# Router ranking in two products, expert rows loaded in halves and turned at once, second layer norm from sum and mean square

## Chip, cores and metric

The kernel runs on one core of one Trainium2 chip. The metric is the device time of one execution in microseconds (us); lower is better. Engines are named as the profile names them: PE (TensorE), DVE (VectorE), ACT (ScalarE), POOL (GpSimd), SP (SyncE, which issues transfers and nothing else here); PEld is PE's weight load.

## What is computed

Two transformer-like blocks on 512 tokens of width 1024, all in float32. The change lies in the first block, between its mixing part and the second block. Cut to that:

```python
xl = post_norm(xl, mod_l[2] * out_l, ln1_g, ln1_b)          # layer_norm(ALPHA * x + y)
hl = modulate(xl, mod_l[3], mod_l[4])                       # input of the experts
# hier_moe: 4 groups of 8 experts
grp = argmax(hl @ w_rg + b_rg)                              # group of each token
top_v, top_i = top_k(le[grp], 2)                            # its two experts
w = p_grp * softmax(top_v)
order = argsort(flat_e)                                     # 1024 (token, expert) pairs by expert
y = swiglu(rows of each expert, w_eg[e], w_eu[e], w_ed[e])
yl = segment_sum(y * w)                                     # sum of each token's two rows
xl = post_norm(xl, mod_l[5] * yl, ln2_g, ln2_b)
# second block: x + 0.5 * swiglu(rms_norm(x)), mixing, x + 0.5 * swiglu(rms_norm(x))
```

`layer_norm` subtracts the mean over the 1024 features and divides by the root of the mean squared deviation plus 1e-5.

## The kernel before, in words

**Layout.** The residual `XT` lies features by tokens: 8 tiles of 128 features x 512 tokens. One tile operation is therefore 128x512. A product in full precision is made of three products of split operands (`HTh`/`HTl`, `HLB`): high x high, high x low, low x high (L582 to L584).

**Weights.** Weights come in tiles of 512 KB through a ring (`Weights`). SP loads them into 4 slots `raw`, and during the expert stage into 5 more, `more` (`lend`, `take_back`). ACT makes the high half of a tile (`ring.hi`, L291), DVE the low half (`ring.lo`, L302), four tiles ahead of PE. A slot is free again when DVE has made the low half, and SP waits for that.

**Order.** Each engine runs its own list of instructions in order, with semaphore waits. The functions `pe_...`, `act_...`, `dve_...` and `pool_...` of one stage are written separately; the order in each function is the order on that engine.

**End of the mixing part** (`*_branches`, last loops). For the eight output tiles `wo`, PE makes the product, DVE adds it to `XT`, and the first layer norm and the router's logits are gathered beside it. `moved(k)` subtracts the mean from tile k on DVE (L2215); POOL then multiplies each tile by the reciprocal deviation `RA` (L2749, signal `xn`); ACT makes from it `HF`, the experts' input (L1570), and the scaled residual (L1572).

**Router** (`*_router`). PE turns the logits (L984). DVE finds the group, the two experts and their one-hot sum `ohs` (L2248 to L2283). PE ranks the pairs in each expert: for token tile i, the strictly lower triangle `sU` times `ohs[i]` plus `ones` times all earlier tiles, and the counts (`rank`, L991 and L994: 14 products of 32 columns). DVE turns ranks into blocks and slots (L2288 to L2346), with one more product (L1004). Meanwhile PE turns `HF` into rows (L680), ACT copies them (L1577) and stores them in DRAM (`H2`, shown as h_scratch). The result `ix` holds the rows that POOL gathers for each expert. SP waits for the last store of `H2` and then loads the five `more` tiles.

**Experts** (`*_experts`). For expert j PE turns the gathered rows `XG` (L1019), makes the gate and up products (L1048 to L1050) and the down product of the expert before (L1030 to L1032). POOL gathers two experts ahead (L2759) and scatters the results to `YD` (y_scratch, L2768). A conditional part for overfull experts follows.

**Combine** (`*_combine`). POOL waits for the last scatter and loads `YD` back in four transfers of 1 MB into `YI` (L2788). For each token tile ACT scales the first row (L1639) and DVE adds the scaled second one (L2406). When all four are done, PE turns the rows (L1072) and DVE adds them to `XT` (L2410) and sums the tiles (L2099). One product with a matrix of 1/1024 gives the mean (L870), DVE subtracts it (L2105), the squares of the centred tiles are added in pairs and go through four products (L854), ACT makes the reciprocal root (L1450, L1452), and DVE, ACT and DVE make the input of the feed-forward part, tile by tile (L2418, L1648, L1650, L2426).

**Feed-forward part** (`*_ffn`). 2 x 11 pairs of products, each pair 48 matmuls. The sum of squares for its RMS norm is made on ACT and POOL (L1660, L2796); `pe_rms` (L864) waits for it behind the first pair.

Of the kernel before, what the change touches and what calls it, by code (L numbers as in the profile page):

```python
# [11 lines left out]
ALU = mybir.AluOpType  # L12
# [8 lines left out]
NRAW = 4  # L21
# [282 lines left out]
def build(nc, I, outT, counted):  # L304
# [5 lines left out]
    with ctx:  # L310
# [22 lines left out]
        y_in = [signal(f"y_in{i}", 16) for i in range(4)]  # L333
# [140 lines left out]
        YL = here("YL", [128, 4, 1024])  # L474
# [52 lines left out]
        PRD = rc(4, 2, 32)  # L527
        LE = rc(NOV, 32)
# [318 lines left out]
        def pe_statistics(i):  # L847

            bank = psum.take(pe, ("square", i))

            def sums():
                for j in range(4):
                    pe.wait_ge(*dve_out.when(("square", i, j)))
                    mm(bank[:, :], K("o1024"), TMP[2 + j % 2][:, :], start=(j == 0), stop=(j == 3)).then_inc(  # L854
                        *pe_out.next(("square", i, j)))
                    yield

            return sums()

# [6 lines left out]

        def pe_norm(i):
            bank = psum.take(pe, ("mean", i))
            pe.wait_ge(*dve_out.when(("mean", i)))
            mm(bank[:, :], K("o1024"), SQ[:, :], start=True, stop=True).then_inc(*pe_out.next(("mean", i)))  # L870
            squares = pe_statistics(i)
            for j, _s in enumerate(squares):
                if j == 2:
                    psum.give(("mean", i), dve_out, ("centred", i, 7))
            psum.give(("square", i), act_out, ("ln", i))
# [104 lines left out]
        def pe_router():  # L980
# [7 lines left out]
            pe.wait_ge(*dve_out.when("ohs"))  # L988
            for i in range(4):
                for j in range(i + 1):  # L990
                    mm(bank[:, i * 32:(i + 1) * 32], K("sU") if j == i else K("ones"), ohs[:, j, :],  # L991
                       start=(j == 0), stop=(j == i))
            for j in range(4):
                ins = mm(bank[:, 128:160], K("ones"), ohs[:, j, :], start=(j == 0), stop=(j == 3))  # L994
            ins.then_inc(*pe_out.next("rank"))
# [70 lines left out]

        def pe_combine():
            for k in range(8):
                bank = psum.take(pe, ("yl", k))
                pe.wait_ge(*dve_out.when(("yl", 3)))  # L1070
                for i in range(4):
                    ins = transpose(bank[:, cols(i)], YL[:, i, cols(k)], K("ident"))  # L1072
# [381 lines left out]
        def act_squares(i, k, signal, done):  # L1454

            if k % 2:
                return
# [1617 lines left out]
```

## Time and profile before

| | us |
|---|---|
| median of 3 runs | 2786.14 |
| the three runs | 2785.41, 2786.14, 2793.68 |
| the profiled execution, its own time | 2790.24 |
| its span | 2788.6 |
| PE busy | 2565.5 (92%) |
| DVE busy | 1686.8 (60%) |
| ACT busy | 1219.4 (44%) |
| POOL busy | 300.7 (11%) |

A page of the profile gives the busy time of each engine, the busy share in 40 slices of the span, the DMA queues and the chain of work that ended last. The busy time of an engine says how much work there is; the chain says which work the end waited for. The timeline shows single instructions with start and duration, and in square brackets how long the engine had been idle before one and what ended that. The windows view sums stretches and has the clock granted to PE, as a share of its full speed.

### The profile page before, as it was taken

To read this page: it belongs to the slowest core of one execution; us is meant where nothing else is said; L and a number is where in the kernel's file an instruction comes from. 1 tells how busy PE (TensorE), PEld (TensorE's weight loads), DVE (VectorE), ACT (ScalarE), POOL (GpSimd) and SP (SyncE) were. 2 spreads that over 40 slices of the span, in tenths; PEclk is the share of its full clock that TensorE was granted. 3 is DMA by queue.
4 is the path that set the end of the run, shared out by engine and by line. 5 is a ranking of instruction groups with operands and counts; after the bars stand their busy time and mean duration, and the time that the engine had idled before them with its cause. 6 is when DMAs were issued, how large, how long until landed. Compare 5 with 4: busy or idle time off the path is not lost.

```text
span 2788.6 us, 30655 instructions
## 1 busy us (share of the span) xinstructions
PE 2565.5 (92%) x12058; PEld 2033.4 (73%) x12058; DVE 1686.8 (60%) x2315; ACT 1219.4 (44%) x1640; POOL 300.7 (11%) x261
## 2 busy tenths in 40 slices
PE   5999898897899959999999948999999998999999
PEld 3867667586778747888888835888887766788887
DVE  3476575857645758999999955434443555543442
ACT  2322323222335448888888835222243544422221
POOL 0010111102122321111111001000023000100000
PEclk9999999999899969999999968999999978999999
DMA  6224242322346329999999941232232110232322
GB/s 262 89 69 154 68 140 99 119 94 69 104 147 204 122 101 327 359 366 363 365 370 364 352 156 61 81 110 97 76 126 69 53 38 23 76 101 80 114 77 82
DMA packets 144885, 427.13 MB, mean 153 GB/s; under 512 B 21152, under 2 KB 35744, under 8 KB 143840
## 3 DMA queue, kind: packets, MB, share of 16 engines
q1 hardware_dynamic: 118560, 373.24, 38.3%
q0 software_dynamic: 13504, 26.64, 2.8%
q10 hardware_dynamic: 12672, 25.24, 2.5%
q8 instruction: 97, 1.59, 0.2%
q14 instruction: 52, 0.43, 0.0%
HBM read 414.55 MB, written 35.65 MB: 161 GB/s over the span
## 4 chain that ended last, share of the span: by engine, by line
PE 75%; DVE 13%; ACT 6%; DMA 3%; issue 2%; POOL 1%; ACTq 0%; SPq 0%; POOLq 0%; DVEq 0%
PE bank L582 16%; PE bank L584 16%; PE bank L583 15%; PE bank L1048 4%; PE bank L1050 4%; PE bank L1049 4%; PE bank L1032 2%; PE bank L1030 2%; PE bank L1031 2%; DVE CA L1999 2%; DVE tmp L1893 2%; ACT HLB L291 1%; DVE HLB L302 1%; DMA early<-in_wada 1%; PE bank L1019 1%
## 5 line engine op out<-in xcount | busy, mean ns | idle before, releaser
L302 DVE TENSOR_TENSOR HLB<-raw,HLB 128x1024 fp32r<-128x1024 f32 x470 | 565.5, 1215 | 503.5 <-ACT HLB L291 502.7
L291 ACT ACTIVATE HLB<-raw 128x1024 fp32r<-128x1024 f32 x470 | 473.6, 1018 | 352.5 <-PE bank L584 287.6
L582 PE MATMUL bank<-HTh,HLB 128*128 128x512 f32 x1320 | 538.0, 408 | 28.3 <-DVE HLB L302 11.2
L584 PE MATMUL bank<-HTh,HLB 128*128 128x512 f32 x1320 | 524.5, 397 | 0.0
L583 PE MATMUL bank<-HTl,HLB 128*128 128x512 f32 x1320 | 521.9, 395 | 0.0
L582 PEld LDWEIGHTS bank<-HTh,HLB 128*128 128x128 f32 x1320 | 252.5, 191 | 106.6 <-issue 33.6
L584 PEld LDWEIGHTS bank<-HTh,HLB 128*128 128x128 f32 x1320 | 251.7, 191 | 58.0
L583 PEld LDWEIGHTS bank<-HTl,HLB 128*128 128x128 f32 x1320 | 252.4, 191 | 55.4 <-issue 2.0
L302 DVE TENSOR_TENSOR HLB<-more,HLB 128x1024 fp32r<-128x1024 f32 x210 | 250.6, 1222 | 16.1 <-ACT HLB L291 15.4
L291 ACT ACTIVATE HLB<-more 128x1024 fp32r<-128x1024 f32 x210 | 218.8, 1065 | 38.1 <-PE bank L1050 28.1
L1048 PE MATMUL bank<-HLB,XGh 128*128 128x512 f32 x512 | 206.3, 403 | 1.9 <-DVE XGl L2375 1.9
L1050 PE MATMUL bank<-HLB,XGh 128*128 128x512 f32 x512 | 203.8, 398 | 0.0
L1049 PE MATMUL bank<-HLB,XGl 128*128 128x512 f32 x512 | 203.6, 398 | 0.0
L584 PE MATMUL bank<-FAh,HLB 128*128 128x512 f32 x352 | 138.9, 395 | 0.0
L583 PE MATMUL bank<-FAl,HLB 128*128 128x512 f32 x352 | 138.9, 395 | 0.0
L582 PE MATMUL bank<-FAh,HLB 128*128 128x512 f32 x352 | 138.9, 394 | 0.0
L1048 PEld LDWEIGHTS bank<-HLB,XGh 128*128 128x128 f32 x512 | 97.1, 190 | 24.6 <-DVE XGl L2375 2.5
L1050 PEld LDWEIGHTS bank<-HLB,XGh 128*128 128x128 f32 x512 | 97.0, 189 | 23.5
L1049 PEld LDWEIGHTS bank<-HLB,XGl 128*128 128x128 f32 x512 | 97.1, 190 | 22.2
L1030 PE MATMUL bank<-HLB,GTh 128*128 128x512 f32 x256 | 104.1, 407 | 2.0 <-DVE GTl L2397 2.0
L1032 PE MATMUL bank<-HLB,GTh 128*128 128x512 f32 x256 | 101.9, 398 | 0.0
L1031 PE MATMUL bank<-HLB,GTl 128*128 128x512 f32 x256 | 101.6, 397 | 0.0
(502 smaller groups left out, 4202.3 us busy)
## 6 DMA issues: line engine op xcount, KB each, us to landing
raw<-in_f SPq DMA_DIRECT2D x120, 512.0 KB, 3.3
more<-in_eg SPq DMA_DIRECT2D x74, 512.0 KB, 5.9
more<-in_eu SPq DMA_DIRECT2D x71, 512.0 KB, 6.4
more<-in_ed SPq DMA_DIRECT2D x65, 512.0 KB, 5.6
raw<-in_ed SPq DMA_DIRECT2D x63, 512.0 KB, 5.9
raw<-in_eu SPq DMA_DIRECT2D x57, 512.0 KB, 6.2
raw<-in_eg SPq DMA_DIRECT2D x54, 512.0 KB, 6.0
raw<-in_wada SPq DMA_DIRECT2D x40, 512.0 KB, 4.1
```

Source lines behind the costliest of these rows:

```text
L291: self.nc.scalar.activation(hi, raw, ACT.Copy).then_inc(*self.w_hi.next(n))
L302: self.nc.vector.tensor_tensor(lo, raw, hi.bitcast(F32), ALU.subtract).then_inc(*self.w_lo.next(n))
L582: mm(bank, ah, bh, start=(start and i == 0), stop=False)
L583: mm(bank, ah, bl, start=False, stop=False)
L584: ins = mm(bank, al, bh, start=False, stop=(stop and i == n - 1))
L1030: mm(bs[n][:, :], GTh[i][:, k, :], w.hi[:, 0, cols(4 * n, 4)], start=(k == 0), stop=False)
L1031: mm(bs[n][:, :], GTl[i][:, k, :], w.hi[:, 0, cols(4 * n, 4)], start=False, stop=False)
L1032: ins = mm(bs[n][:, :], GTh[i][:, k, :], w.lo[:, 0, cols(4 * n, 4)], start=False, stop=(k == 3))
L1048: mm(bank[:, :], XGh[i][:, k, :], w.hi[:, kk, :], start=(k == 0), stop=False)
L1049: mm(bank[:, :], XGl[i][:, k, :], w.hi[:, kk, :], start=False, stop=False)
L1050: ins = mm(bank[:, :], XGh[i][:, k, :], w.lo[:, kk, :], start=False, stop=(k == 7))
L1893: ins = scalar_tensor_tensor(out=E4[h % 2][d][:, cols(c)], in0=psum[("sums", g, h, d)][:, cols(c)], scalar=src[:, c, hh:hh + 1], in1=K("mF ...
```

## The change

Five things are changed.

1. **Ranking.** DVE makes sums of the one-hot tiles before each token tile (`earlier`), and PE needs two products: `ones` times `earlier` (160 columns) and `sU` times `ohs` (128 columns).
2. **Work moved in the router.** The split of one weight tile (`ring.hi`, `ring.lo`) leaves the last `wo` step. Four of eight `moved` operations, all eight `xn` operations (from POOL to DVE) and that split on DVE stand behind `earlier` and ahead of the read of the ranks. ACT's scaled residual moves behind the rows' stores. SP loads the `more` tiles only after the first gather has landed.
3. **Expert rows.** SP, not POOL, loads them, in 8 transfers of 512 KB: first the features 0 to 511 of all four token tiles, then the others. SP issues them ahead of the feed-forward tiles 4 to 7. ACT scales both rows, POOL adds them, and PE turns each half once it is there.
4. **Second layer norm.** PE sums the eight tiles of `XT` itself by eight products with 1/1024; the squares of the uncentred tiles are added on POOL in three groups and take three products; the variance is mean square less squared mean.
5. **RMS of the first feed-forward part.** `pe_rms` stands behind the second pair of products instead of the first.

```diff
@@ pe_router
-            pe.wait_ge(*dve_out.when("ohs"))
-            for i in range(4):
-                for j in range(i + 1):
-                    mm(bank[:, i * 32:(i + 1) * 32], K("sU") if j == i else K("ones"), ohs[:, j, :],
...
+            pe.wait_ge(*dve_out.when("earlier"))
+            mm(bank[:, 0:160], K("ones"), earlier[:, :, :].rearrange("p a b -> p (a b)"), start=True, stop=False)
+            mm(bank[:, 0:128], K("sU"), ohs[:, :, :].rearrange("p a b -> p (a b)"), start=False, stop=True).then_inc(
@@ pe_combine
+            mean, square = psum.take(pe, ("mean", 2)), psum.take(pe, ("square", 2))
...
+            for k in range(4):
+                turn(k)
+            for k in range(4):
+                row(k)
+            squares("0123", TMP[0], start=True)
+            for k in range(4, 8):
+                turn(k)
+            for k in range(4, 7):
+                row(k)
+            squares("45", TMP[4])
+            row(7).then_inc(*pe_out.next(("mean", 2)))
+            squares("67", TMP[2], stop=True).then_inc(*pe_out.next(("square", 2)))
@@ pe_ffn
-                    if half == 0 and f == 0:
+                    if half == 0 and f == (name == "n1"):
                         pe_rms(name)
@@ act_branches, dve_branches (the same edit with ring.lo)
             for c in range(8):
-                ring.hi(act, "wo", c)
+                if c < 7:
+                    ring.hi(act, "wo", c)
@@ act_router
             for k in range(8):
-                act.wait_ge(*pool_out.when(("xn", k)))
+                act.wait_ge(*dve_out.when(("xn", k)))
                 activation(HF[:, k, :], XT[:, k, :], ACT.Identity, scale=hg_[:, k:k + 1], bias=hb_[:, k:k + 1]).then_inc(
                     *act_out.next(("h2f", k)))
-                activation(XT[:, k, :], XT[:, k, :], ACT.Identity, scale=ag_[:, k:k + 1], bias=ab_[:, k:k + 1]).then_inc(
...
             activation(wt[:, :, 0:5], wt[:, :, 0:5], ACT.Exp).then_inc(*act_out.next("w"))
+            for k in range(8):
+                activation(XT[:, k, :], XT[:, k, :], ACT.Identity, scale=ag_[:, k:k + 1], bias=ab_[:, k:k + 1]).then_inc(
+                    *act_out.next(("ln1", k)))
@@ act_combine
+            for i in range(4):
+                weigh(0, i)
+            weigh(1, 0)
+            weigh(1, 1)
+            square(0)
+            square(1)
+            weigh(1, 2)
+            square(2)
+            weigh(1, 3)
+            for k in range(3, 8):
+                square(k)
             act_logs()
@@ dve_router
+            own()
+            nc.vector.tensor_copy(earlier[:, 1, :], ohs[:, 0, :]).then_inc(*dve_out.next())
+            tensor_tensor(earlier[:, 2, :], ohs[:, 0, :], ohs[:, 1, :], ALU.add).then_inc(*dve_out.next())
...
+            for k in range(9):
+                if k < 8 and k > 3:
+                    moved(k)
+                if k:
+                    dve.wait_ge(*dve_out.when(("moved", 1, k - 1)))
+                    tensor_tensor(XT[:, k - 1, :], XT[:, k - 1, :], RA[:, :], ALU.mult).then_inc(
+                        *dve_out.next(("xn", k - 1)))
+            ring.lo(dve, "wr", 0)
             dve.wait_ge(*pe_out.when("rank"))
@@ dve_combine
+            for k in range(2):
+                centre(k)
+            dve.wait_ge(*pe_out.when(("square", 2)))
+            dve.wait_ge(*act_out.when(("mm", 2)))
+            tensor_tensor(TMP[1][:, :], psum[("square", 2)][:, :], TMP[5][:, :], ALU.subtract).then_inc(
+                *dve_out.next(("var", 2)))
+            for k in range(2, 5):
+                centre(k)
@@ pool_combine
+            for i in range(4):
+                both(0, i)
+            both(1, 0)
+            both(1, 1)
+            add(0, 1)
+            both(1, 2)
+            add(0, 2)
+            both(1, 3)
+            add(0, 3, ("squares", "0123"))
+            add(4, 5, ("squares", "45"))
+            add(2, 7, ("squares", "67"))
@@ SP's order
-        sp.wait_ge(*h2_out.when(3))
+        sp.wait_ge(*gathered[0].when(0))
...
+        ring.load(sp, ring.start_of("f11", 0) + NRAW)
+        sp.wait_ge(*scattered.when(31))
...
+        for h in range(2):
+            for i in range(4):
+                nc.sync.dma_start(YI[:, i, :, cols(4 * h, 4)], rows[i][:, :, cols(4 * h, 4)]).then_inc(
+                    *y_in[4 * h + i].next("y"))
         ring.load(sp, len(ring.plan.keys))
```

`turn(k)` waits for POOL's sum of its half and makes four transposes; `row(k)` waits for DVE's update of `XT` tile k and adds one product of 128x512 to the mean; `weigh(h, i)` is two ACT copies with a scale, 128x512 each; `both(h, i)` and `add(...)` are POOL additions of 128x512; `centre(k)` is DVE's subtraction of the mean.

## Rows read from the trace of the kernel before

**Rows 1.** The page: the chain that ended last, share by engine.

```profile
PE 75%; DVE 13%; ACT 6%; DMA 3%; issue 2%; POOL 1%; ACTq 0%; SPq 0%; POOLq 0%; DVEq 0%
```

**Rows 2.** The chain around the router: start us, us, what.

```profile
983.49 1.07 ACT HLB L291
...
985.72 0.75 DVE XT L2191
...
1026.53 8.32 DMA XG<-h_scratch,ix
...
1038.34 0.80 PE bank L1048
```

**Rows 3.** Timeline of the router: start, us, engine, line, operation [idle before].

```profile
993.67 14.09 POOL L2749 TENSOR_TENSOR XT<-XT,RA 128x512 f32<-128x512 f32 x8 [17.15 <-ACT RA L1452]
...
994.24 3.68 DVE L2215 TENSOR_TENSOR XT<-XT,tmp 128x512 f32<-128x512 f32 x6
...
995.12 0.64 PE L984 MATMUL bank<-km,LGT 36*128 36x36 f32 x4 [3.31 <-ACT LGT L1566]
...
998.04 0.31 DVE L2248 TENSOR_TENSOR rt<-bank,pr 128x144 f32<-128x144 f32 x1
...
1000.40 1.24 DVE L2262 TENSOR_TENSOR rt<-km,rt 128x128 f32<-128x128 f32 x1
...
1007.83 0.49 DVE L2280 TENSOR_TENSOR rt<-km,rt 128x128 f32<-128x128 f32 x2
...
1014.70 5.74 PE L680 MATMUL bank<-km,HF 128*128 128x128 f32 x32
1014.93 0.19 DVE L2288 COPY rt<-bank 128x32 f32<-128x32 f32 x1 [6.11 <-PE bank L994]
...
1022.00 0.33 ACTq L1581 DMA_DIRECT2D h_scratch<-HR  x1
```

**Rows 4.** From issue to landing: the 32 gathers, then the four stores of `H2`.

```profile
DMA to landing us min/median/max: 3.0/7.0/8.5
...
DMA to landing us min/median/max: 2.6/2.6/2.6
```

**Rows 5.** Expert stage: SP's waits in it, and a window of 100 us.

```profile
SPq L258 <- DVE HLB L302: 444.3, 366, 12.5
...
1130.00:1230.00 100.00, 100.00 (x463) 81.41 (x462) 91.42 (x89) 84.48 (x100) 14.81 (x12) 1.00 0.98 362
```

**Rows 6.** The chain in the combine: start us, us, what.

```profile
1631.33 1.64 POOL YI L2788 x3
1632.97 16.54 DMA YI<-y_scratch
...
1680.32 0.70 DVE XT L2418
```

**Rows 7.** Timeline of the combine and what follows it.

```profile
1652.05 6.21 PE L1072 MATMUL bank<-km,YL 128*128 128x128 f32 x32 [25.25 <-DVE YL L2406]
...
1664.01 2.04 PE L870 MATMUL bank<-SQ,km 128*128 128x512 f32 x2 [5.75 <-DVE sm L2414]
...
1681.05 0.81 ACT L1648 ACTIVATE HTh<-XT,sm 128x512 fp32r<-128x512 f32 x1 [0.76 <-DVE XT L2418]
...
1696.02 8.39 POOL L2796 TENSOR_TENSOR SQ<-SQ,tmp 128x512 f32<-128x512 f32 x6 [0.80 <-ACT tmp L1660]
...
1704.47 1.58 PE L864 MATMUL bank<-SQ,km 128*128 128x512 f32 x2 [4.36 <-POOL SQ L2796]
```

**Rows 8.** Windows: us, busy PE, PEld, DVE, ACT, POOL, PE clock, DMA share, GB/s.

```profile
10.00:20.00 10.00, 2.19 (x21) 0.40 (x16) 0.00 (x0) 0.00 (x0) 0.00 (x0) 1.00 1.00 413
...
1657.00:1658.00 1.00, 1.00 (x11) 1.00 (x9) 0.97 (x2) 0.00 (x0) 0.00 (x0) 0.89 0.00 0
...
1661.00:1662.00 1.00, 0.00 (x0) 0.00 (x0) 0.97 (x3) 0.00 (x0) 0.00 (x0) 0.50 0.00 0
...
1706.00:1708.00 2.00, 2.00 (x7) 1.52 (x6) 1.17 (x2) 1.86 (x3) 0.00 (x0) 0.50 0.67 209
```

More of the change, by code:

```diff
@@ L527, in build @@
         PRD = rc(4, 2, 32)
+        earlier = rc(5, 32)
         LE = rc(NOV, 32)
@@ L845, in pe_scan @@
             return gating
[L847 to L858, printed above, removed]
         def pe_rms(name):
@@ L865, in pe_rms @@
             psum.give(("square", name), act_out, ("ln", name))
[L867 to L875, printed above, removed]
         def pe_branches(gating):
@@ L987, in pe_router @@
             bank = psum.take(pe, "rank")
-            pe.wait_ge(*dve_out.when("ohs"))
-            for i in range(4):
-                for j in range(i + 1):
-                    mm(bank[:, i * 32:(i + 1) * 32], K("sU") if j == i else K("ones"), ohs[:, j, :],
[L992 to L995, printed above, removed]
+            pe.wait_ge(*dve_out.when("earlier"))
+            mm(bank[:, 0:160], K("ones"), earlier[:, :, :].rearrange("p a b -> p (a b)"), start=True, stop=False)
+            mm(bank[:, 0:128], K("sU"), ohs[:, :, :].rearrange("p a b -> p (a b)"), start=False, stop=True).then_inc(
+                *pe_out.next("rank"))
             psum.give("rank", dve_out, "rk")
@@ L2229, in dve_branches, with moved @@
             tensor_tensor(LGT[:, :], LGT[:, :], RA[0:36, :], ALU.mult).then_inc(*dve_out.next("lgs"))
-            for k in range(2, 8):
+            for k in range(2, 4):
                 moved(k)
+        def moved(k):
+            dve.wait_ge(*act_out.when(("mu", 1)))
+            dve.wait_ge(*dve_out.when(("h2", k)))
+            tensor_tensor(XT[:, k, :], XT[:, k, :], TMP[1][:, :], ALU.subtract).then_inc(*dve_out.next(("moved", 1, k)))
         def dve_router():
@@ L2244, in dve_router @@
             nc.vector.memset(t32, 0.0).then_inc(*dve_out.next())
-            ring.lo(dve, "wr", 0)
+            nc.vector.memset(earlier[:, 0, :], 0.0).then_inc(*dve_out.next())
             own()
@@ L2745, in pool_branches @@
                                         ALU.add).then_inc(*pool_out.next(("sumsq", 1, k)))
-            pool.wait_ge(*act_out.when(("rs", 1)))
-            for k in range(8):
-                pool.wait_ge(*dve_out.when(("moved", 1, k)))
-                nc.gpsimd.tensor_tensor(XT[:, k, :], XT[:, k, :], RA[:, :], ALU.mult).then_inc(
-                    *pool_out.next(("xn", k)))
             pool_out.mark("routed")
@@ L2781, in pool_combine, with both, add @@
         def pool_combine():
-            pool.wait_ge(*scattered.when(31))
-            pool.wait_ge(*pe_out.when("experts"))
-            pool.wait_ge(*dve_out.when("experts"))
-            pool.wait_ge(*act_out.when("experts"))
-            rows = YD.rearrange("(t p k) n -> t p k n", p=128, k=2)
-            for i in range(4):
-                nc.gpsimd.dma_start(YI[:, i, :, :], rows[i]).then_inc(*y_in[i].next("y"))
+            def both(h, i):
+                y = [YI[:, i, k, cols(4 * h, 4)] for k in range(2)]
+                pool.wait_ge(*act_out.when(("yw", h, i)))
+                nc.gpsimd.tensor_tensor(y[0], y[0], y[1], ALU.add).then_inc(*pool_out.next(("yl", h, i)))
+            def add(a, k, key=None):
+                pool.wait_ge(*act_out.when(("sq", 2, k)))
+                pool.wait_ge(*pool_out.now())
+                nc.gpsimd.tensor_tensor(TMP[a][:, :], TMP[a][:, :], SQUARE[k][:, :], ALU.add).then_inc(
+                    *pool_out.next(key))
+            for i in range(4):
+                both(0, i)
[8 more added lines that the diff above has]
+            add(2, 7, ("squares", "67"))
         def pool_rms(name):
```

106 lines of the change are left out of this document (48 added, 58 removed).

## Prediction

> **What bounds the kernel now.** First the page's chain by engine: three quarters of the end is PE's own work [rows 1]; only the stretches in which PE stands still can give time back. The chain in order of time shows two such stretches where the change works: the router, from the last `wo` product to the first expert product at 1038.34 [rows 2], and the combine, from the last scatter to the feed-forward part. In the router the reader is to see DVE small operations, a ranking on PE for which DVE is idle 6.11 us, and a gather of 8.32 us [rows 2, 3]; in the combine a load of 16.54 us, then 28.3 us from the first transpose to the first product with the reciprocal deviation (1652.05 to 1680.32), then 4.36 us of waiting for the RMS sum [rows 6, 7]. Between them PE is busy for 100 of 100 us [rows 5], so a start of the experts that comes earlier brings their end forward by as much, if weights keep up.
>
> **Router, step by step.** (a) The split of a tile that left the last `wo` step stood on the chain: ACT from 983.49, DVE free for the update at 985.72 [rows 2]. Gone: -2.2 us. (b) Ahead of the logits DVE did six `moved` in 3.68 us [rows 3], 0.61 each. Two are left, ending at 995.5; the transposed logits are there at 995.12 + 0.64 = 995.8, and DVE took them up at 998.04 [rows 3]: -2.2. (c) POOL's eight `xn` run from 993.67 to 1007.76 [rows 3]. In them a DVE operation on 128x128 takes 1.24 us (four in a row like it, L2262 to L2269); the pair of the same shape behind them takes 0.49 together [rows 3]. Without POOL, four times 1.0; for one copy and one cast beside them another 1.0 (my estimate by the same ratio): -5.0. (d) For the ranking DVE was idle for 6.1 [rows 3]. Now DVE has its own work in that place: four `earlier` operations at some 0.25, twelve tile operations (four `moved`, eight `xn`) at 0.61 = 7.3, and one weight split of 1.2 (985.72 - 983.49 - 1.07, rounded up) [rows 2, 3]; 9.6 in all. PE's two products are 288 columns; at 2.04 us for 512 [rows 7] that is 1.2 us and hidden. +3.5. Sum at the read of the ranks: -5.9, so it comes at 1009.0.
>
> From there to the gather nothing changes (1014.93 to 1026.53, 11.6 us): gather at 1020.6 [rows 2, 3]. The other path to it is `H2`. The last `xn` ends at 1009.0 - 1.2 = 1007.8, `HF` 0.8 later [rows 7]; from the first transpose to the last store were 1022.00 - 1014.70 = 7.3 [rows 3], and a store landed 2.6 after its issue [rows 4]: 1018.5. It is next in line, 2.1 us from being late. ACT's eight moved operations take 0.8 each at most [rows 7], 6.4, and end before the gather lands.
>
> (e) The gather ran beside five weight tiles and took 8.32; the shortest of the 32 took 3.0 [rows 2, 4]. With SP held until it has landed I take 3.1: -5.2. Behind SP's new wait stand the five `more` tiles, and behind them all later ones. PE starts 3.5 us after landing (1038.34 - 1034.85) with eight tiles at hand; a tile is six matmuls, and 463 take 100 us [rows 5], so these last 10.4 us. Five tiles and the second gather, 3.1 MB at 413 GB/s [rows 8], need 7.6 us and a start-up of some 3. Cost zero, if so; if the cover is gone, 1.3 us a tile. Router: -5.9 - 5.2 = **-11.1**, bounds -8 and -13.
>
> **Combine.** The load of 4 MB began at 1631.33 and its last quarter took 16.54 us [rows 6], beside 2 MB of feed-forward tiles that SP had issued. Now SP issues the halves first; behind its wait for the last scatter stand feed-forward tiles 4 to 7, used by the third pair of products only, over 30 us later: no cost. The first 512 KB need some 3 us (the shortest gather [rows 4]), each further one 1.25 (at 413 GB/s, which transfers of 2 KB rows reached in [rows 8]): half one is in at 1637.9, half two at 1642.9. ACT's two scalings take 0.72 each (between 0.6 and 0.81 [rows 7]), POOL's addition 1.40 (8.39/6 [rows 7]): PE turns half one from 1641.5, not 1652.05.
>
> The Trainium skill's DMA: Bandwidth & Descriptors (Where 436 GB/s comes from) speaks against this: for HBM to SBUF it has some 358 GB/s as binding. By that a half would need 5.9 instead of 5.1 us, and the sum would be 0.8 worse. The row at 413 GB/s decides; the trace disagrees.
>
> From here POOL is the longest engine. After the four additions of half one it has seven more (four of half two, three of squares) before the first product of squares: 9.8 us and 0.6 of waiting for ACT's squares, to 1652.0; I add 0.8, since its additions took 1.76 each beside DVE in the router (14.09/8 [rows 3]). PE meanwhile turns four tiles (0.78 each, 6.21/8 [rows 7]) and adds four rows, then waits some 2.5 us. One such product is 2.04 us at half clock [rows 7] and half of that at full clock. The clock rose some 5 us after transposes began at 1652.05, and by 1661, 2.7 us after they ended, it was at half again [rows 7, 8]. I take the squares at half clock (2.0 less an overlap), four transposes 3.1, then four rows and two products of squares at 1.04, so the mean is there near 1663 and the last product near 1664. Copy of the mean 0.7, two `centre` 1.2, variance 0.7, then three more `centre` 1.9 (beside logarithm and root, 1.4) and signals of 0.3: the first `n2m` is due at 1667.8, not 1680.32 [rows 6]: -12.5. Bounds: all of PE's products at half clock, +5.0; all at full clock, -2.0.
>
> Behind it DVE has three `centre` of 0.61 among its work per tile, two operations of 0.69 and 0.75; ACT, with two of some 0.71, had set the pace. The three delay it by 0.9 before it catches up: +0.9. Then `pe_rms`: it stood at 1704.47, with PE idle for 4.4 us before it, and what followed ran at half clock [rows 7, 8], for some 3 us with its own product: a loss of 1.8 (my estimate). With the second pair of products (11.0 us) ahead of it POOL's sum is long ready: -6.2. What is late next: the second pair needs no RMS, two banks and two tiles that are ready; ACT and DVE then have two pairs to catch up with at some 7 us against PE's 11: no cost. Combine: -12.5 + 0.9 - 6.2 = **-17.8**, bounds -12 and -21.
>
> **Sum.** 2790.24 - 11.1 - 17.8 = 2761.3 for the profiled execution. That one lies 4.1 above the median of the three; the same step from the median gives **2757**.
>
> **Rivals.**
> - *POOL and the low clock rule the combine.* Eight scalings pass to ACT and eight additions to POOL, which takes 1.40 to 1.76 for what DVE did as 0.64. At 1.76 the eleven additions on the way cost 4 more (less the 0.8 counted), and half clock 5.0: 2757 + 8 = 2765. For it: the clock stayed low from 1661 on, with PE busy in bursts. Against: PE has dense work here. 0.17.
> - *The start starves.* Each of the five tiles comes late by its own 1.3 us: 2757 + 7 = 2764. Against: eight tiles at hand, and an expert stage in which SP waited 366 times for a slot, never PE for a tile [rows 5]. 0.10.
> - *The gather is no shorter or `H2` is late.* Then the change doesn't do what it says there: 2757 + 5.2 = 2762, up to 2764. For it: the median gather took 7.0 [rows 4]. 0.09.
> - *Slower: the expert stage lives on its lead.* It moves 362 GB/s at a DMA share of 0.98 [rows 5]. If that is all that it can draw, the lead of five tiles never comes back and PE waits at each of 32 experts; from 0.9 us each (29/32) the whole gain is gone, at 1.3 it is 2757 + 42 = 2799. Against: 413 GB/s elsewhere [rows 8] and the slot waits. 0.03.
>
> **Chances.** Forecast 0.60 with 2751 to 2761, the rivals as above, 0.01 left. About 0.3%, 8.4 us, is what a measurement of this kernel can tell from no change. Faster 0.94 (all but the last rival and a small part of the others), same 0.03, slower 0.03. The range takes in the bounds (2752 to 2766), the rivals on the same side, and, since single executions lay 8 us apart, reaches from 2748 to 2771.
>
> **What would show each step.** (a, b) The logits' first DVE operation at 993.6 to 993.9. (c) L2262's kin at 0.25 us. (d) A DVE block of 12 tile operations behind `ohs`, the read of the ranks near 1009. (e) A gather of 3 to 3.5 us and no PE wait for weights in the first two experts. Combine: the first transpose 10.5 us after SP's first issue, a PE wait of 2 to 3 us for POOL ahead of the squares, 36 to 37 us from that issue to `n2m`, no idle PE ahead of `pe_rms`. Wrong would be: a gather above 5 us, POOL operations above 1.8 us, a low clock through all rows, or waits of PE for weight tiles between the experts.

## The result, and the profile after

The changed kernel takes 2757.85 us in the median (four executions, 2754.88 to 2766.26) against 2787.93 for the kernel before (four, 2785.41 to 2793.68): a ratio of 0.9894, 95% interval 0.9866 to 0.9922. A second comparison on one chip gave 2755.35 (six executions) and 2790.47 (eleven): 0.9879, 0.9859 to 0.9900. The profiled execution is the slowest of the first four, 2766.26 us with a span of 2765.0; the profiled one of before has a span of 2788.6, so these two lie only 23.6 us apart.

The page of the changed kernel: the chain by engine. It answers [rows 1].

```profile
PE 75%; DVE 12%; ACT 6%; DMA 3%; issue 2%; POOL 2%; ACTq 0%; SPq 0%; DVEq 0%; POOLq 0%
```

The shares hardly move: 30 us are 1% of the span. The time has to be read stretch by stretch, from one fixed instruction to the next. The timeline of the router in the changed kernel (start, us, engine, line, operation, idle before), to be held against [rows 3]:

```profile
994.81 0.31 DVE L2235 TENSOR_TENSOR rt<-bank,pr 128x144 f32<-128x144 f32 x1 [0.23 <-PE bank L961]
...
1008.27 2.35 DVE L302 TENSOR_TENSOR HLB<-raw,HLB 128x1024 fp32r<-128x1024 f32 x2
...
1010.54 0.18 DVE L2290 COPY rt<-bank 128x32 f32<-128x32 f32 x1
...
1018.43 2.91 PE L977 MATMUL bank<-rt 128*128 128x78 f32 x16 [3.88 <-DVE rt L2339]
...
1023.05 1.10 POOL L2768 DMA_INDIRECT XG<-h_scratch,ix  x1 [44.92 <-DVE rt L2225]
...
1027.30 1.75 SPq L258 DMA_DIRECT2D more<-in_eg  x4
...
1030.69 0.79 PE L1021 MATMUL bank<-HLB,XGh 128*128 128x512 f32 x1 [1.41 <-DVE XGl L2377]
```

The read of the ranks (L2290) has no idle time ahead of it, where before it had 6.11 us [rows 3]. SP issues the `more` tiles only once the gather has landed (1027.30).

The timeline of the combine in the changed kernel, to be held against [rows 6, 7]:

```profile
1620.83 6.15 SPq L2941 DMA_DIRECT2D YI<-y_scratch  x8
...
1625.86 1.33 ACT L1633 ACTIVATE YI<-YI,wk 128x512 f32<-128x512 f32 x2 [4.38 <-DMA YI<-y_scratch]
...
1630.66 1.34 ACT L1633 ACTIVATE YI<-YI,wk 128x512 f32<-128x512 f32 x2 [0.22 <-DMA YI<-y_scratch]
...
1632.08 1.26 POOL L2794 TENSOR_TENSOR YI<-YI 128x512 f32<-128x512 f32 x1 [0.29 <-ACT YI L1633]
...
1633.49 3.65 PE L1049 MATMUL bank<-km,YI 128*128 128x128 f32 x16 [16.92 <-POOL YI L2794]
...
1643.55 1.76 PE L1059 MATMUL bank<-tmp,km 128*128 128x512 f32 x2 [2.95 <-POOL tmp L2799]
1645.11 3.00 PE L1049 MATMUL bank<-km,YI 128*128 128x128 f32 x16
...
1647.94 2.74 PE L1055 MATMUL bank<-XT,km 128*128 128x512 f32 x6
...
1656.68 0.68 DVE L2430 TENSOR_TENSOR XT<-XT,RA 128x512 f32<-128x512 f32 x1
```

Half one is in 9.8 us after the first issue (1630.66), PE turns it at 1633.49, waits 2.95 us for POOL's squares, and the first `n2m` (DVE's first multiplication of an `XT` tile by the reciprocal deviation, L2430) comes at 1656.68, 35.85 us after SP's first issue; before it was 48.99 [rows 6].

Last, `pe_rms` in the changed kernel, and a POOL operation on `KT` in the second block's mixing part, first of the kernel before, then of the changed one. It is the second of four such operations, lies behind all that the change touches and serves as the end mark; below it is called the `KT` mark (`after_again`'s expectation calls it the last `KT`):

```profile
1687.85 1.02 PE L851 MATMUL bank<-SQ,km 128*128 128x512 f32 x2
```

```profile
2142.80 1.26 POOL L2814 TENSOR_TENSOR KT<-tmp,tmp 128x512 f32<-128x512 f32 x1 [3.69 <-DVE tmp L2482]
```

```profile
2113.47 1.27 POOL L2838 TENSOR_TENSOR KT<-tmp,tmp 128x512 f32<-128x512 f32 x1 [3.69 <-DVE tmp L2496]
```

The stretches, in us, of the two profiled executions:

| stretch | before | after | moved | forecast |
|---|---|---|---|---|
| start to the last `wo` product | 983.4 | 985.0 | +1.6 | 0 |
| to DVE's first logits operation | 14.65 | 9.86 | -4.8 | -4.4 (a, b) |
| to the end of `ohs` | 10.61 | 5.39 | -5.2 | -5.0 (c) |
| to the read of the ranks | 6.28 | 10.34 | +4.1 | +3.5 (d) |
| to the gather's issue | 11.60 | 12.51 | +0.9 | 0 |
| to the first expert product | 11.81 | 7.64 | -4.2 | -5.2 (e) |
| to the last scatter | 590.35 | 587.77 | -2.6 | 0 |
| to the first load of rows | 2.64 | 2.37 | -0.3 | 0 |
| to the first transpose | 20.72 | 12.66 | -8.1 | -10.2 |
| to the first `n2m` | 28.27 | 23.19 | -5.1 | -2.3 |
| to the `KT` mark | 462.48 | 456.79 | -5.7 | -5.3 |
| to the end | 645.8 | 651.5 | +5.7 | 0 |

What the change works on adds up to -9.2 - 0.3 - 13.1 - 5.7 = **-28.3**; the forecast was -28.9. The other rows, -2.6 + 1.6 + 5.7 = +4.7, are code that the change leaves alone.

### The profile page after: what moved, and what is told of

The parts are those of the page before. It is cut to its first block, busy times and chain, and to the rows that moved or that the text cites. A ratio compares the mean times of both kernels' runs of the same rounds, so it can differ in the third digit from the quotient of the medians.

```text
span 2765.0 us, 30650 instructions
## 1 busy us (share of the span) xinstructions
PE 2566.0 (93%) x12046; PEld 2035.8 (74%) x12046; DVE 1670.5 (60%) x2310; ACT 1228.3 (44%) x1658; POOL 301.3 (11%) x262
## 4 chain that ended last, share of the span: by engine, by line
PE 75%; DVE 12%; ACT 6%; DMA 3%; issue 2%; POOL 2%; ACTq 0%; SPq 0%; DVEq 0%; POOLq 0%
PE bank L582 16%; PE bank L584 16%; PE bank L583 15%; PE bank L1021 4%; PE bank L1023 4%; PE bank L1022 4%; PE bank L1005 2%; PE bank L1003 2%; PE bank L1004 2%; DVE CA L2012 2%; DVE tmp L1906 2%; ACT HLB L291 2%; DVE HLB L302 1%; DMA early<-in_wada 1%; PE bank L992 1%
```

## Is the rest chance? The two parts alone, and the kernel again

**`router_only`** and **`combine_only`** are the kernel before with one part of the diff each: points 1 and 2 of the change for the one, points 3 to 5 for the other. **`after_again`** is the changed kernel itself.

> The kernel before with the router part alone (ranking in two products, xn on DVE, moved and ln1 reordered, the last wo split dropped, SP held until the first gather has landed); the combine as before. Theory (the router part is worth what its stretch shows): from the last wo product to the first expert product 45 to 46.5 us instead of 54.94, so 9 faster, plus up to 3 in the expert stage if that shortening (590.4 to 587.8) belongs to the change: 2776 to 2779 against 2788. Rival (the gain of the router is given back later, or by the clock): over 2782. If the expert stage takes 590 here, its 2.6 us were the clock's and not the change's.

> The kernel before with the combine part alone (rows loaded in halves on SP's queue, weighed on ACT, added on POOL, second norm from sum and mean square, pe_rms behind the second pair); the router as before. Theory: from the load's first issue to the first n2m 36 us instead of 49.0, and 5 to 6 more by pe_rms: 18 to 20 faster, 2768 to 2770. The two parts then add up to the whole (30). Rival (the parts share something, such as the phase of the clock): the sum of the two gains is off from 30 by over 4.

> The changed kernel itself beside the kernel before on this chip, for more executions of both. Theory (28.3 us by the stretches that the change works on, the rest is chance of the clock elsewhere): 28 faster, with the four stretches within 0.5 us of the first profile (router 45.7, experts 587.8, load to n2m 35.9, n2m to the last KT 456.8), and the expert stage at 590.4 in some executions whatever the kernel. Rival (the 30.1 of the first medians is the truth, and the change gains 2 more in a place not named): over 30.

`router_only`: 2784.69 (10 executions) against 2792.07 (13) for the kernel before, ratio 0.9976 (0.9961 to 0.9991), 7.4 us between the medians. `combine_only`: 2768.76 (4), ratio 0.9898 (0.9870 to 0.9927), 23.3 us. The whole change, again: 0.9879, 35.1 us. The gather and the first expert product in `router_only`; its last `wo` product ends at 991.30:

```profile
1029.44 1.10 POOL L2768 DMA_INDIRECT XG<-h_scratch,ix  x1 [44.99 <-DVE rt L2237]
...
1037.16 0.79 PE L1045 MATMUL bank<-HLB,XGh 128*128 128x512 f32 x1 [1.41 <-DVE XGl L2389]
```

The router takes 45.86 us here (45.74 in the changed kernel, 45.94 in its second profile). In `combine_only` the load to `n2m` takes 35.87 (35.85 and 35.26), and `n2m` to the `KT` mark 456.83 (456.79 and 456.80). So the stretches repeat to some tenths of a us, but for the landing of the loads (the first transpose of half one came 11.6 to 12.9 us after the first issue) and for the product of the blocks (L977, 1.98 to 3.23 us). By the stretches the two parts are independent: 9.1 and 0.3 + 13.1 + 5.7 make up the 28.3.

The medians don't fit this as well. The 95% intervals are 2.5 to 10.9 us for the router part, 20.4 to 36.3 for the combine part and 27.9 to 39.3 for both. They hold the 9.1 and the 28.3 but miss the 19.1 by 1.3 us. By its total `after_again` came to its rival (over 30 faster), though its named stretches were within 0.3 us of the first profile but for the load to `n2m`, 0.6 shorter. `router_only` missed its 2776 to 2779 and lies above its rival's 2782, though its stretch is the one expected; the kernel before stood at 2792 beside it and not at 2788. Some of this may be scatter: three medians of the kernel before were 2787.93, 2790.47 and 2792.07. Whether the code outside the stretches also runs faster as a rule behind the new combine is open: nearly every kernel here has one profile.

The 2.6 us of the expert stage don't belong to the change. The stage took 590.4 us in the kernel before, 590.4 and 590.3 in two variants of the changed kernel below, and 587.4 to 588.2 in all eleven others (the kernel before with the combine part, and with the load moved, among them). Windows behind the first expert (us, PE, PEld, DVE, ACT, POOL busy, PE clock, DMA share, GB/s), first of the kernel before, then of the changed one:

```profile
1053.00:1060.00 7.00, 5.18 (x17) 4.03 (x18) 5.03 (x6) 4.06 (x6) 0.99 (x1) 0.76 0.75 266
```

```profile
1046.00:1053.00 7.00, 5.31 (x24) 4.27 (x25) 5.47 (x7) 5.14 (x8) 0.99 (x1) 1.00 0.75 270
```

PE has short waits in this place in both. In the one the granted clock falls for a part of it, in the other it stays. The two variants with 590, `splits_later` and `turns_first`, have 0.76 at the same place of their stage too, and `router_only` has 1.00.

The same holds for the end. The changed kernel and the variant `xn_on_pool` (below) reach the `KT` mark at 2113.47 and 2113.48, run the same code from there, and need 651.5 and 637.8 us. Windows 63 us further on, first of the changed kernel, then of the variant:

```profile
2176.00:2181.00 5.00, 5.00 (x19) 3.59 (x18) 4.08 (x13) 0.38 (x2) 0.00 (x0) 0.50 0.00 0
2181.00:2186.00 5.00, 5.00 (x25) 5.00 (x25) 0.33 (x1) 0.61 (x2) 0.00 (x0) 0.50 0.00 0
```

```profile
2176.00:2181.00 5.00, 5.00 (x38) 4.29 (x36) 3.75 (x11) 0.71 (x2) 0.00 (x0) 0.94 0.00 0
2181.00:2186.00 5.00, 3.84 (x18) 1.74 (x18) 2.02 (x5) 1.97 (x5) 0.00 (x0) 1.00 0.00 0
```

In one execution this piece of mixing runs at 0.50, 1.2 GHz, with 19 matmuls in 5 us, in the other near full clock with 38. Over all fourteen profiles (the changed kernel has two, the kernel before and its two parts, and nine variants) the code up to the last `wo` product took 983.4 to 991.3 us, and that behind the `KT` mark 637.6 to 651.5. In the three with the old combine this end took 645.5 to 645.8, in the eleven with the new one 644.0 in the mean: too little a difference, over this scatter, to account for the medians.

## Router: what the gather and POOL cost

**`gather_beside`**: SP's wait of the kernel before, in the changed kernel.

```diff
-        sp.wait_ge(*gathered[0].when(0))
+        sp.wait_ge(*h2_out.when(3))
```

> The changed kernel with SP's wait for the first gather put back to the wait for the last H2 store, so that the five more tiles are drawn beside the gather. Theory: the gather takes 7.5 to 8.5 us instead of 4.15 and the first expert product comes 3.5 to 4.3 later; the whole is 3 to 4 slower than the changed kernel, 2761 to 2762. Rival (a starved start: the tiles that come later now cost as much as the gather gains): within 1 us of the changed kernel. Third: the five tiles are issued only with ACT's routed mark at the same moment as the gather, so it slows by half only: 2 slower.

The `ln1` operations, the product of the blocks, the gather and the `more` tiles in this variant:

```profile
1020.50 5.73 ACT L1573 ACTIVATE XT<-XT,sm 128x512 f32<-128x512 f32 x8
...
1021.77 1.98 PE L977 MATMUL bank<-rt 128*128 128x78 f32 x16 [3.28 <-DVE rt L2339]
...
1025.46 1.10 POOL L2768 DMA_INDIRECT XG<-h_scratch,ix  x1 [44.07 <-DVE rt L2225]
1026.30 2.02 SPq L258 DMA_DIRECT2D more<-in_eg  x4
```

The gather in its chain of waits, and then the issue of these tiles in the kernel before, 1.7 us ahead of the gather at 1026.53 [rows 2]:

```profile
1025.46 5.82 DMA XG<-h_scratch,ix
```

```profile
1024.86 1.75 SPq L258 DMA_DIRECT2D more<-in_eg  x4
```

The gather takes 5.82 us, against 4.15 in the changed kernel and 8.32 before [rows 2]. My main expectation, 7.5 to 8.5, was wrong; the third one came out. SP also waits for ACT's part of the router, and since ACT's eight `ln1` stand at its end now (until 1026.23), the five tiles go out at 1026.30, 0.8 us behind the gather's issue and not ahead of it. So of the 4.2 us that term (e) gained, SP's new wait is worth 1.7; the other 2.5 were there without it, and the timeline puts them down to the moved `ln1`, which no variant moved back by itself. The median of this variant (2768.54, four executions, expected 2761 to 2762) is 13 us above the changed kernel's second one; by its stretches it is 1.7, less 0.9 for a product of the blocks at full clock (1.98 us). The starved start is refuted: the expert stage takes 588.1 here with the tiles early and 587.8 with them late.

**`xn_on_pool`**: the eight products with `RA` back on POOL, all else as in the changed kernel.

```diff
-                if k:
-                    dve.wait_ge(*dve_out.when(("moved", 1, k - 1)))
-                    tensor_tensor(XT[:, k - 1, :], XT[:, k - 1, :], RA[:, :], ALU.mult)...
+            for k in range(8):                      # in POOL's list
+                pool.wait_ge(*dve_out.when(("moved", 1, k)))
+                nc.gpsimd.tensor_tensor(XT[:, k, :], XT[:, k, :], RA[:, :], ALU.mult)...
```

> The changed kernel with the eight xn back on POOL, where the kernel before had them. Theory (an addition on POOL slows the small DVE operations beside it): from the first logits operation to the end of ohs 9.5 to 10.6 us instead of 5.4, each of the four 128x128 operations 1.0 or more instead of 0.25; DVE is rid of eight operations (4.9 us) behind ohs, so the rank read moves by only -0.5 to +1. Rival (the small operations were slow for another reason in the kernel before, such as waits for their own results): 5.4 us stay, and the rank read comes 4.4 us earlier.

POOL and DVE in this variant. POOL works until 999.30, then waits for `moved`, which stands behind `ohs` here, until 1003.98:

```profile
992.58 6.72 POOL L2759 TENSOR_TENSOR XT<-XT,RA 128x512 f32<-128x512 f32 x4 [14.52 <-ACT RA L1451]
...
996.93 1.24 DVE L2249 TENSOR_TENSOR rt<-km,rt 128x128 f32<-128x128 f32 x1
...
998.20 1.24 DVE L2252 TENSOR_TENSOR rt<-rt 128x128 f32<-128x128 f32 x1
...
999.48 0.23 DVE L2254 TENSOR_SCALAR rt<-rt 128x128 f32<-128x128 f32 x1
999.74 0.29 DVE L2256 TENSOR_TENSOR rt<-rt 128x128 f32<-128x128 f32 x1
...
1003.22 4.62 DVE L2218 TENSOR_TENSOR XT<-XT,tmp 128x512 f32<-128x512 f32 x4
...
1007.77 4.48 DVE L302 TENSOR_TENSOR HLB<-raw,HLB 128x1024 fp32r<-128x1024 f32 x2
```

The mechanism shows within one timeline: two of the four 128x128 operations start while POOL works and take 1.24 us, the other two start after it has stopped and take 0.23 and 0.29; when POOL is back, `moved` takes 1.16 instead of 0.61. From the logits to `ohs` it is 7.58 us: 2.2 more than without POOL, not the 4 to 5 that I expected, since POOL covers only half of the stretch. With the 9.80 from there to the rank read (10.34 in the changed kernel) the ranks come 1.6 later, where I had expected at most 1, and the router takes 46.44. DVE is rid of eight operations (4.9 us) behind `ohs` but gains only 0.5 by it, since beside POOL the four `moved` take 4.62 us and the two splits 4.48 instead of 2.35. The move of `xn` is thus worth 1.6 us at the ranks against this variant.

The Trainium skill (SBUF — State Buffer, SBUF: two separate sides) has this as an exclusive lock on a pair of ports that DVE and GpSimd share: whoever starts first has it for its whole instruction, and a DVE operation needs it if it has two SBUF inputs, against a GpSimd operation that reads SBUF, or runs in a two-port mode. The rows agree, and `dve_adds` below shows the other side: a DVE operation that has one of its two tiles in PSUM isn't slowed.

**`splits_later`**: the two weight splits that DVE does ahead of the rank read go behind the last operation ahead of the product of the blocks.

```diff
-            ring.lo(dve, "wr", 0)
             dve.wait_ge(*pe_out.when("rank"))
...
+            ring.lo(dve, "wr", 0)
             dve.wait_ge(*pe_out.when("blocks"))
```

> The changed kernel with DVE's two weight splits, which stand ahead of its read of the ranks, put behind the last operation ahead of the blocks product, for which DVE is idle 3.1 us. Theory: the two splits (2.35 us) go under that wait, the gather is issued 2.3 us earlier and the first expert product too: router 43.4 us instead of 45.7. Rival (the path through H2 is next and was only some 1.3 us from being late, or the two raw tiles that come free later starve the start): gain under 1.3 us, or PE waits for weights in the first experts.

```profile
1019.12 2.35 DVE L302 TENSOR_TENSOR HLB<-raw,HLB 128x1024 fp32r<-128x1024 f32 x2
1020.36 1.46 SPq L258 DMA_DIRECT2D raw<-in_eu  x2
1023.37 1.10 POOL L2768 DMA_INDIRECT XG<-h_scratch,ix  x1 [42.10 <-DVE eidi L2357]
```

The ranks come 2.3 earlier and the router takes 43.55 us, 2.2 less, as the theory had it, though the gather takes 4.8 here with the two raw tiles loading beside it. PE waits for no weights in the first two experts. The expert stage took 590.4 in this execution; in `best`, with the same edit, 587.4, and the granted clock at its start was that of the other slow stages (above), so I put this down to the clock too.

## Combine: queue, halves, order, engine

**`queue_only`** and **`whole_loads`** take the load apart: the kernel before with its four loads moved to SP's queue, and the changed kernel with whole transfers, its work still done by halves. These two, `xn_on_pool`, `splits_later`, `turns_first` and `dve_adds` have one execution each (2784.08, 2754.52, 2752.58, 2762.63, 2753.13, 2757.13 us in this order); they are read by their stretches alone.

```diff
# queue_only, against the kernel before
-                nc.gpsimd.dma_start(YI[:, i, :, :], rows[i]).then_inc(*y_in[i].next("y"))
+        ring.load(sp, ring.start_of("f11", 0) + NRAW)
+        ...
+            nc.sync.dma_start(YI[:, i, :, :], rows[i]).then_inc(*y_in[i].next("y"))
# whole_loads, against the changed kernel
-        for h in range(2):
-            for i in range(4):
-                nc.sync.dma_start(YI[:, i, :, cols(4 * h, 4)], rows[i][:, :, cols(4 * h, 4)])...
+        for i in range(4):
+            nc.sync.dma_start(YI[:, i, :, :], rows[i])...
```

> The kernel before with one edit: the four loads of the expert rows (still 1 MB each) are issued on SP's queue behind the first four feed-forward tiles and ahead of the later ones, instead of on POOL's beside them. Read from the stretch from the last scatter to the first n2m, 51.6 us in the kernel before and 38.2 in the changed one. Theory (the queue alone gives a small part, the halves and the second norm the rest): the last load lands 15 to 16 us after its first issue instead of 18.2, the stretch is 48.5 to 49. Rival (the feed-forward tiles beside the load were what made it slow): the load is in after 11 us or less, the stretch under 45. Third (no effect of the queue): 51 to 52.

> The changed kernel with the expert rows loaded in four whole transfers of 1 MB on SP's queue; all else, the halves of the work included, unchanged. Theory (halves are worth what lies between the landing of half one and of the whole): all is in 15.6 us after the first issue as now, the first transpose comes 18.4 us after it instead of 12.7, the first n2m 41 to 42 instead of 35.9. Rival (POOL's additions rule, and whole rows of 4 KB land sooner than rows of 2 KB): n2m at 37 to 38.

The first transpose in `queue_only`, whose first load was issued at 1631.22:

```profile
1631.22 2.10 SPq L2913 DMA_DIRECT2D YI<-y_scratch  x4
...
1646.42 5.84 PE L1072 MATMUL bank<-km,YL 128*128 128x128 f32 x30 [19.46 <-DVE YL L2406]
```

And in `whole_loads`, with the issue, ACT's last wait for a load, and the transpose:

```profile
1619.84 1.98 SPq L2940 DMA_DIRECT2D YI<-y_scratch  x4
...
1631.90 3.78 ACT L1633 ACTIVATE YI<-YI,wk 128x512 f32<-128x512 f32 x6 [1.11 <-DMA YI<-y_scratch]
...
1634.72 3.65 PE L1049 MATMUL bank<-km,YI 128*128 128x128 f32 x16 [19.15 <-POOL YI L2794]
```

Issued ahead of the later feed-forward tiles, all 4 MB are in 12.1 us after the first issue in `whole_loads` and 12.7 in `queue_only`, against 18.2 before (1649.51 - 1631.33 [rows 6]). Both of my expectations had 15 to 16. `queue_only` fell between theory and rival; `whole_loads` came to its rival (`n2m` at 37 to 38). The way to `n2m` is now taken apart, in us from the first issue:

| | to the first transpose | from there to `n2m` | together |
|---|---|---|---|
| before | 20.7 | 28.3 | 49.0 |
| `queue_only` | 15.2 | 28.3 | 43.5 |
| `whole_loads` | 14.9 | 23.2 | 38.1 |
| changed | 12.7 | 23.2 | 35.9 |

The queue is worth 5.5 us, the second norm with its new places (and the work by halves) 5.4, and the halved transfers 2.2, or 2.0 to 3.2 against the other profiles with the same work up to there.

Why so little for the halves: the rates while the load runs (GB/s in 40 slices of 0.55 us from 1618), first in the changed kernel, with rows of 2 KB, then in `whole_loads`, with rows of 4 KB:

```profile
GB/s 15 0 0 16 7 0 0 63 201 264 156 238 331 339 361 395 398 410 372 276 268 287 298 380 402 387 391 410 410 417 432 421 421 425 410 425 410 425 372 149
```

```profile
GB/s 0 8 15 0 0 194 104 447 447 432 372 417 477 432 432 358 447 462 447 417 372 447 462 417 372 402 432 402 439 395 447 395 432 142 0 0 0 0 0 0
```

The halves start at 156 to 264 GB/s, come to 395 only some 4 us on and fall below 300 once more for 2 us; whole transfers are at 447 in their third slice. SP needs 6.15 us to issue eight halves (0.61 each in the median, 0.43 for a whole one). So half one is in at 9.8 us after the first issue, and the whole load in the other variant at 12.1.

The rates bear on the figure of the Trainium skill that the prediction weighed (DMA: Bandwidth & Descriptors, Where 436 GB/s comes from): 358 GB/s don't bind here: the load in whole transfers moved 358 to 477 in each full slice, in most over 400. The trace disagrees, as [rows 8] did.

**`rms_first`**: `pe_rms` back behind the first pair of products.

```diff
-                    if half == 0 and f == (name == "n1"):
+                    if half == 0 and f == 0:
```

> The changed kernel with pe_rms back behind the first pair of products of the first feed-forward part. Theory: PE stands idle for 4 to 4.6 us ahead of it and loses up to 1.8 by the clock: 4.4 to 6.2 slower, 2762 to 2764. Rival (what waits there is only moved: banks or the divided tile stall PE at the third pair instead, so the position is worth nothing): within 1 us.

```profile
1686.31 1.98 PE L851 MATMUL bank<-SQ,km 128*128 128x512 f32 x2 [4.36 <-POOL SQ L2820]
1687.30 1.42 PE L582 MATMUL bank<-HTh,HLB 128*128 128x512 f32 x1
```

Idle for 4.36 us and then at half clock: 1.98 us for the product where it takes 1.02 in the changed kernel. `n2m` to the `KT` mark is 463.08 instead of 456.79: 6.3 us, at the upper end of the theory. Nothing was moved on to a later wait. The median is 2775.84 (four executions, ratio 0.9930), 20 us above the changed kernel's second one, where I had expected 2762 to 2764; its stretches don't show the rest.

**`turns_first`**, **`dve_adds`** and **`best`** ask what bounds the combine now.

```diff
# turns_first: PE, and both(1, 3) ahead of add(0, 2) on POOL
-            squares("0123", TMP[0], start=True)
             for k in range(4, 8):
                 turn(k)
+            squares("0123", TMP[0], start=True)
# dve_adds: with the same order on PE, the additions on DVE
-                nc.gpsimd.tensor_tensor(y[0], y[0], y[1], ALU.add)...
+                scalar_tensor_tensor(out=y[0], in0=y[1], scalar=wk[:, i, 1:2], in1=y[0], ...)
# best: dve_adds and splits_later, and for tiles 6 and 7
-            add(2, 7, ("squares", "67"))
+                mm(square[:, :], K("o1024"), TMP[k - 4][:, :], start=False, stop=(k == 7))
```

> The changed kernel with PE's four turns of half two ahead of its product of the squares 0 to 3, and POOL's four additions of half two ahead of its additions of squares 2 and 3. Theory (POOL's order and PE's wait for it are on the path): PE no longer idles 2.95 us ahead of the squares and the turns come 2 to 3 us earlier, the first n2m 31 to 32 us after the load's first issue instead of 35.9. Rival (it is the number of additions on POOL that counts, not their order): 34.5 to 36.

> The changed kernel with the same order on PE, and the eight additions of expert rows on DVE, which stands idle there, as one weighted addition each (ACT then weighs one row of a pair, not both); POOL has the squares only. Theory (POOL is the longest engine of the combine, as forecast): the first transpose at 11.3 us instead of 12.7, half two is turned from 17, the first n2m at 27 to 28.5 instead of 35.9. Rival (half two's landing, at about 15.6 us, or the squares on POOL rule): 30 or more.

> A version meant to beat both: the additions on DVE and the turns first, PE adding up the squares of tiles 6 and 7 itself instead of waiting for POOL's addition, and DVE's two weight splits behind the last operation ahead of the blocks product. Theory: n2m at 26 to 27.5 instead of 35.9, and the router 43.5 instead of 45.7: 10 to 12 faster than the changed kernel, 38 to 42 faster than the one before. Rival (what is saved in the router is lost in the expert stage, 590.4 instead of 587.8): 8 to 9 faster than the changed kernel.

From the first issue to `n2m`: `turns_first` 31.9, `dve_adds` 30.2, `best` 31.1, against 35.9. In `turns_first`, PE's second turns and the squares:

```profile
1645.04 1.94 PE L1049 MATMUL bank<-km,YI 128*128 128x128 f32 x16 [0.48 <-POOL YI L2794]
...
1647.71 1.13 PE L1059 MATMUL bank<-tmp,km 128*128 128x512 f32 x2 [0.74 <-POOL tmp L2799]
```

That is 4.0 less, as expected, but only 3.0 of it is the order's: from the first transpose to `n2m` it is 20.2 instead of 23.2. PE's wait is 0.74 us instead of 2.95, and its squares take 1.13 instead of 1.76, at a granted clock of 1.00 instead of 0.50. The other 1.0 is half one, which landed after 8.8 us instead of 9.8, within the scatter of the landings. To move the eight additions to DVE brings only 1.6 more. In `dve_adds`:

```profile
1640.43 1.40 DVE L2416 SCALAR_TENSOR_TENSOR XT<-bank,mod,XT 128x512 f32<-128x512 f32 x2
1640.61 4.70 POOL L2813 TENSOR_TENSOR tmp<-tmp,tmp 128x512 f32<-128x512 f32 x3 [16.37 <-ACT tmp L1638]
...
1641.75 2.42 DVE L2411 SCALAR_TENSOR_TENSOR YI<-YI,wk 128x512 f32<-128x512 f32 x2
...
1644.52 1.91 PE L1049 MATMUL bank<-km,YI 128*128 128x128 f32 x16
```

Beside POOL's squares, DVE's additions (L2411, both inputs in SBUF) take 1.21 us each instead of 0.75, and POOL's 1.57 instead of 1.27; `moe` (L2416, one input in PSUM) takes 0.70 there as ever. From 1644.52 PE is then busy without a break until its last product: the combine has become PE's. Half two's path is close behind, since its last addition ended at 1644.17. So `best`, which gives PE one more product to save POOL an addition, gains nothing by it: 19.4 us from the first transpose to `n2m`, against 19.0 in `dve_adds`. My expectation of 26 to 28.5 for both was wrong, since it had left out what PE still had to do; in `dve_adds` the rival's number (30 or more) came out.

I had expected `best` to be 10 to 12 us faster than the changed kernel. It takes 43.0 us for the router and 31.1 for the combine, 7.1 less than the changed kernel's second profile in these two. Yet its median is 2759.89 (six executions, 2754.63 to 2764.15), ratio 0.9890 (0.9872 to 0.9908), against 2755.35 and 0.9879 for the changed kernel beside it. It is no proven gain: its mean granted clock is 0.950 to 0.955, that of the changed kernel 0.953 to 0.958, and in the two profiles the code behind the `KT` mark takes 645.4 against 637.8. Whether a shorter combine draws the clock down later or this was chance is open; no run here tells it apart.

## Why the prediction was right

It said 2757, and 28.9 us for the profiled execution; the median is 2757.85, and the stretches that the change works on give 28.3. That the median fits to 1 us is luck: the kernel before had medians 4 us apart, and outside the stretches two executions can differ by 14. The terms, in its own order:

- **(a), (b) Split and fewer `moved`: right.** 4.8 for 4.4.
- **(c) POOL beside DVE: right in the kernel**, 5.2 for 5.0. `xn_on_pool` shows the mechanism, and 2.2 us of the size.
- **(d) The ranking: right, 4.1 for 3.5.** Two splits stand ahead of the read, 2.35 us, where I had put one of 1.2; the rest of DVE's block was shorter than I had it.
- **Ranks to gather: 0.9 missed.** I had this as unchanged. The product of the blocks took 2.91 us in the changed kernel, the granted clock being 0.64 over these 3 us, and 1.98 in `gather_beside` at 1.00: in code that waits for DVE PE's clock may be either.
- **(e) The gather: too good by 1.1.** 4.15 us for 3.1: I had taken the shortest of 32. The second gather is issued 1.4 us behind and runs beside it. That nothing starves was right. What I had not seen is that `ln1`, moved behind, holds back SP by itself; over half of the gain was there without the wait that I had it from.
- **Load to `n2m`: right in sum, 13.1 for 12.5, by two errors that cancel.** The first transpose came 12.7 us after SP's first issue, not 10.5 (my working even has 10.2, 1641.5): I had the first landing after 3 us and 413 GB/s from there; it was 4.9 us, and the 2 KB rows needed some 4 us to come near that rate. The row that I had this from doesn't show it: of the 4.13 MB in its window, 1.15 moved in 2 KB packets, the others in packets of 8 and 16 KB. From there to `n2m` I had 26.0 and it was 23.2. The first squares came 10.1 us behind the first transpose, where I had 11, since POOL's additions take 1.27 (I had 1.40, then 0.8 more). From there to `n2m` I had 15.0 and it was 13.1, about half of that since PE's products at full clock follow each other every 0.86 us (L1055), where I had priced each at 1.04. The clock was as forecast, 0.50 for the squares and most of the transposes behind them (1644 to 1647), 1.00 from 1648, and so were the PE wait for POOL, 2.95 us, and its place.
- **`centre` and `pe_rms`: right.** 5.7 for 5.3; of it 6.3 by `pe_rms` (`rms_first`), less 0.6.

Of the rivals, a starved start and a late `H2` are refuted; the last store of `H2` took 4.2 us to land instead of 2.6 but was in at 1020.66, 2.4 us ahead of the gather's issue. A low clock in the combine came true in part (0.50 in the first transposes, and from 1644 on for some 3 us), without deciding. That the expert stage lives on its lead, the one mechanism that would have ended on the slower side, is refuted by the equal stages with the tiles early and late.

What the forecast lacked is the size of what lies outside: up to 14 us between executions in code that is the same. Its range went only 4 to 5 us beyond the bounds of the terms.

## To carry to other kernels

Cost a change by the stretch between two fixed instructions, and check it there: most stretches repeated to tenths of a us, while medians of the same kernel over 4, 11 and 13 executions lay 4 us apart. When an operation is moved, look at what else its old place held back or let go: here, by the timeline, ACT's moved `ln1` kept the weight tiles off the gather more than the wait that was put in for it. And when an engine is relieved, count what the next one has to do before you expect the whole gain: the halves, POOL's additions and the direct squares each gave less than their own cost, since loads, and then PE, were next.

## What the runs showed of the hardware

- While POOL adds or multiplies tiles, a DVE 128x128 operation with its inputs in SBUF takes 1.24 us instead of 0.25 to 0.29, a 128x512 one 1.16 to 1.21 instead of 0.61 to 0.75, and the split of a 128x1024 tile 2.24 on average instead of 1.2. With one input in PSUM it keeps its 0.70.
- A load of 512 KB with rows of 2 KB from DRAM lands 4.2 to 4.9 us after its issue when it is the first of a burst (ten profiles), and a burst of eight runs at 156 to 264 GB/s for 2 us near its start; of four of 1 MB with rows of 4 KB the first lands after 4.7 us (5.0 in `queue_only`), and they are at 447 GB/s in the third slice of 0.55 us. SP spends 0.61 us on issuing each of the first, 0.43 on each of the second.
- From one and the same instant on, the same code took 637.8 and 651.5 us; in one window of 5 us in it the granted clock was 0.94 and 0.50.
